# The first block's norms: tiles asked for between the next stage's products, four side by side, and one group of the modulation multiplied inside the norm

## The reference, cut to what matters

```python
def modulate(x, shift, scale): return x * (1.0 + scale) + shift
mods = adaln_modulation(c, ada_w[layer], ada_b[layer])   # silu(c) @ ada_w + ada_b, nine vectors of 1024
x = layer_norm(ALPHA * x + 0.5 * mods[2] * ffn(modulate(x, *mods[0:2])), g0, b0)
x = layer_norm(ALPHA * x + mods[5] * mixer(modulate(x, *mods[3:5])), g1, b1)
x = layer_norm(ALPHA * x + 0.5 * mods[8] * ffn(modulate(x, *mods[6:8])), g2, b2)
```

## Time and profile before

| | us |
|---|---|
| median of 3 runs | 2887.48 (2884.63 to 2893.36) |
| profiled execution | 2885.58 |
| its span | 2883.8 |
| granted clock of TensorE, mean | 0.949 |
| HBM | 348.98 MB read, 121 GB/s over the span |

### The profile page before, as it was taken

The page is one execution under the profiler, slowest core; times in us unless marked ns, Lnnn a source line. Parts: engine busy times, 40 slices in busy tenths (PEclk is TensorE's granted clock), DMA queues, the critical chain, the costliest instruction groups (busy, mean ns, idle before and its releaser), DMA issues.

```text
span 2883.8 us, 43361 instructions
## 1 busy us (share of the span) xinstructions
PE 2680.6 (93%) x16824; PEld 2313.4 (80%) x16824; DVE 1731.7 (60%) x2978; ACT 1260.8 (44%) x2390; POOL 671.8 (23%) x608
## 2 busy tenths in 40 slices
PE   8999997988788999999999988989979999899998
PEld 5887886867776888887888867789978988898888
DVE  5775666778766765556554555565544656346666
ACT  3332326531255333334333345655545575454673
POOL 1111111012134111112111121021134424555224
PEclk9999998998788999998999988999979999899999
DMA  6553441210002543433443422245524434334334
GB/s 252 184 175 115 153 154 44 81 59 2 2 16 74 179 168 127 144 128 117 161 153 124 168 81 74 81 139 184 183 88 135 145 109 133 131 132 139 117 104 138
DMA packets 115868, 352.85 MB, mean 122 GB/s; under 512 B 12752, under 2 KB 14928, under 8 KB 115280
## 3 DMA queue, kind: packets, MB, share of 16 engines
q1 hardware_dynamic: 115664, 350.08, 36.1%
HBM read 348.98 MB, written 1.05 MB: 121 GB/s over the span
## 4 chain that ended last, share of the span: by engine, by line
PE 72%; DVE 12%; ACT 7%; issue 5%; POOL 3%; DMA 1%; SPq 0%; DVEq 0%; ACTq 0%; POOLq 0%
PE ps L1570 20%; PE ps L1572 19%; PE ps L1571 19%; ACT spl L1884 2%; PE ps L1620 2%; DVE spl L2120 1%; DVE big L2330 1%; PE ps L1636 1%; DVE work L2307 1%; PE ps L1838 1%; PE ps L1630 1%; DVE work L2225 1%; ACT big L2061 1%; POOL bigr L2584 1%; PE ps L1581 1%
## 5 line engine op out<-in xcount | busy, mean ns | idle before, releaser
L1570 PE MATMUL ps<-bigr,spl 128*128 128x256 f32 (+1 forms) x3880 | 1344.2, 346 | 69.9 <-issue 21.2
L1571 PE MATMUL ps<-bigr,spl 128*128 128x256 f32 (+1 forms) x3880 | 1313.4, 339 | 0.0
L1572 PE MATMUL ps<-bigr,spl 128*128 128x256 f32 (+1 forms) x3880 | 1312.9, 338 | 0.0
L2120 DVE TENSOR_TENSOR spl<-ring,spl 128x512 fp32r<-128x512 f32 x838 | 678.0, 819 | 652.8 <-ACT spl L1884 650.2
L1884 ACT ACTIVATE spl<-ring 128x512 fp32r<-128x512 f32 x1024 | 623.6, 625 | 763.8 <-PE ps L1572 606.2
L1570 PEld LDWEIGHTS ps<-bigr,spl 128*128 128x128 f32 x3880 | 750.4, 193 | 182.3 <-issue 44.7
L1571 PEld LDWEIGHTS ps<-bigr,spl 128*128 128x128 f32 x3880 | 752.4, 194 | 75.0 <-issue 2.2
L1572 PEld LDWEIGHTS ps<-bigr,spl 128*128 128x128 f32 x3880 | 750.9, 194 | 76.4
L2584 POOL TENSOR_TENSOR bigr<-work,bigr 128x512 fp32r<-128x512 f32 (+1 forms) x200 | 210.8, 1060 | 1026.5 <-ACT bigr L1888 1026.4
L2579 POOL TENSOR_TENSOR spl<-ring,spl 128x512 fp32r<-128x512 f32 x186 | 254.3, 1369 | 361.2 <-ACT spl L1884 360.9
L1888 ACT ACTIVATE bigr<-work 128x512 fp32r<-128x512 f32 (+2 forms) x232 | 120.5, 522 | 317.9 <-DVE work L2202 169.2
(11 more groups left out here) (291 smaller groups left out, 2506.6 us busy)
## 6 DMA issues: line engine op xcount, KB each, us to landing
ring<-w_stream SPq DMA_DIRECT2D x512, 512.0 KB, 3.4
big<-w_stream SPq DMA_DIRECT2D x256, 256.0 KB, 3.0
big<-w_stream SPq DMA_DIRECT2D x16, 512.0 KB, 11.0
X<-x_t SPq DMA_DIRECT2D x2, 1024.0 KB, 13.7
cst<-consts SPq DMA_DIRECT2D x1, 1601.5 KB, 7.3
X<-mem_t SPq DMA_DIRECT2D x1, 1024.0 KB, 5.7
out_t<-X SPq DMA_DIRECT2D x8, 128.0 KB, 2.1
prm<-params SPq DMA_DIRECT2D x1, 252.5 KB, 2.7
```

Source lines behind the costliest of these rows:

```text
L1570: pe.matmul(out, hi, x[0], start=k == 0, stop=False)
L1571: pe.matmul(out, hi, x[1], start=False, stop=False)
L1572: finish(pe.matmul(out, lo, x[0], start=False, stop=k == nk - 1), tile, key if k == nk - 1 else None)
L2120: dve.tensor_tensor(lo_half(h), raw_half(h), hi_half(h), SUB).then_inc(*sig("lo", h, by="lo_dve"))
```

## The change

1. **Side by side.** `pair` becomes `side_by_side` for any number of products. After each norm four products (three in the odd mixer: key 0, query 0 with 256 columns, key 1) advance together by feature tile. The norm is an object, `Norm`; its `between` asks for tile k+1 before the products of k.
2. **Fills.** Five groups of the modulation (0,15), (0,16), (1,7), (1,16), (1,17) leave the background. Each is multiplied as 8 plain fp32 matmuls inside a norm: two before the sums, one between sums and squares, one behind the mean, four behind 1/deviation. Their weights are loaded into the place where `XM`'s low parts will stand, so the first tile's `dual` waits for the last fill.
3. **Product order.** High by high, low by high, and only then high by low, which waits for the input's low part.
4. **Residual** straight from the product's bank on DVE; X is kept multiplied by ALPHA (`first_scale` at the start; `ln_update` with gain and offset times ALPHA). The sums of X are multiplied before those of the squares.
5. **ln_update** one for every four feature tiles of later products instead of eight in a row; in the odd mixer, where no long product follows, all at once.
6. **Odd mixer.** The memory's squares behind the values by token; memory keys and queries regrouped.
7. The silu of a short convolution one convolution later; the square root's table asked for ahead of the sums.

```diff
             def linear(key, bank, free, k, nk, tile, x, need, n):
-                w.all(need, done)
+                for step, u in need:
+                    w.wait_ge(*done("dhi", u))
                 hi, lo = weights(tile)
                 pe.matmul(out, hi, x[0], start=k == 0, stop=False)
-                pe.matmul(out, hi, x[1], start=False, stop=False)
-                finish(pe.matmul(out, lo, x[0], start=False, stop=k == nk - 1), tile, ...)
+                pe.matmul(out, lo, x[0], start=False, stop=False)
+                w.all(need, done)
+                finish(pe.matmul(out, hi, x[1], start=False, stop=k == nk - 1), tile, ...)
...
+            def side_by_side(keys, ws, src, n, between=None, all_=None):
+                all_ = all_ or [banks.get() for _ in keys]
                 for k in range(len(src)):
                     if between:
                         yield from between(k)
                     hi, lo, need = src[k]
+                    for (bank, free, bi), key, w, n in zip(all_, keys, ws, ns):
                         tile = yield from take(w(k))
+                        yield "linear", key, bank, free, k, len(src), tile, (hi[:, 0:n], lo[:, 0:n]), need, n
...
+            class Norm:
+                def tile(self, k):
+                    if k == 0:
+                        yield "ln_sub", u, 0, n, mean[0], [mean[1]] + self.need
+                    if k < KD - 1:
+                        yield "ln_sub", u, k + 1, n, mean[0], [mean[1]] + self.need
+                    yield "ln_mul", u, k, n, r[0], r[1]
+                    yield "ln_mod", u, k, n, m, nxt[0], nxt[1], [nxt[2]] + mfree
+                    t = yield from dual(m[:, 0:n], XM[k][0][:, 0:n], XM[k][1][:, 0:n], self.read[k] + self.after)
+                def between(self, k):
+                    if k == 0:
+                        yield from self.tile(0)
+                    yield from self.tile(k + 1)
...
+                    bs, sfree, si = banks.get()
+                    yield from fill(2)
+                    yield "colsum", us, bs, [(accS, self.s)], n, sfree
+                    yield from fill(1)
+                    c = yield from columns(n, [(accQ, self.q)])
...
+                    yield from fill(1)
                     yield "inverse", u, col[:, 8:8 + nb], col[:, 4:4 + nb]
                     r = yield from root_spread(n, c)
+                    yield from fill(4)
...
+            def fill(l, g, k, bank, free):
+                if k == 0:
+                    w.all(free, done)
+                    w.wait_ge(*done("fill_in", l, g, KD - 1))
+                a = 96 + 4 * k
+                pe.matmul(bank, c4[:, a:a + 128], B((KD + k) * T, T), start=k == 0, stop=k == KD - 1)...
...
             def residual(u, k, n, bank, gt, need, xneed):
-                dve.scalar_tensor_tensor(x, x, ALPHA, t[:, 0:n], MUL, ADD)...
+                for s, a, b in halves(n):
+                    x = Xt[k][:, a:b]
+                    ins = dve.scalar_tensor_tensor(x, bank[:, a:b], gt[:, k, s:s + 1], x, MUL, ADD)
...
             def odd_mixer(xs, ms):
+                yield from headnorm(9, T, "kn", K[1], second)
+                tV = yield from odd_values(xs4, srcv, VK, f0)
                 for k in range(KD):
                     yield from sums.add(MX[k], [("m",)], k == KD - 1)
-                tV = yield from odd_values(xs4, srcv, VK, f0)
                 r, key, ri = yield from sums.finish(D, "eps6")
```

More of the change, by code:

```diff
@@ L461, in spread, with columns @@
                 return b, ("spread", u), bi
-            def columns(n, squares, plain=()):
+            def columns(n, squares):
                 b, free, bi = banks.get()
@@ L599, in ada_vec, with fill_load, fill, fill_end @@
                 yield from total(*prev)
+            def fill_load(l, g, free):
+                bank, bfree, bi = banks.get()
+                for k in range(KD):
+                    if not signals.at:
+                        side.append([("ada_w", (l,), 128 * k, 128, 512 * g, 512, 0)])
+                    yield "fill_load", l, g, k, pos["a"], free
+                    pos["a"] += 1
+                for k in range(KD):
+                    filler.append(("fill", l, g, k, bank, bfree))
+                filled[:] = [l, g, bank, bi]
+            def fill(n):
+                for _ in range(n):
+                    if filler:
+                        yield filler.pop(0)
+            def fill_end():
+                if not filled:
+                    return
+                l, g, bank, bi = filled
+                filled.clear()
+                row, rfree, ri = tmps.get()
+                yield "fill_row", l, g, row, bank, rfree
+                banks.give(bi, ("ada_row", l, g))
+                def turned():
+                    b, free, bi2 = banks.get()
+                    yield "fill_turn", l, g, row, b, free
+                    tmps.give(ri, ("ada_t", l, g))
+                    yield "ada_mod", l, g, 2, b
+                    banks.give(bi2, ("mod", l, g))
+                later.append(turned)
             def conditions(l, i):
@@ L631, in layer_norm, with next_norm @@
+            def next_norm(n, keep, sums, g, b, nxt):
+                norm = Norm(n, keep, g, b, nxt)
+                norm.after = [("fill", *filled[0:2], KD - 1)] if filled else []
+                yield from norm.chain(sums)
+                assert not filler
+                later.append(fill_end)
+                return norm.xs, norm
+            def layer_norm(n, sums, g, b):
                 mean, r = yield from sums.finish(D, "eps5")
                 u = new()
-                xs, ms = [("xs", u, k) for k in range(KD)], []
+                xs = [("xs", u, k) for k in range(KD)]
+                following = Sums(n, both=False, need=[pos["colsum"]])
@@ L827, in even_mixer @@
                 for n, m in enumerate((0, 4, 1, 5, 2, 6, 3, 7, 8, 9, 10, 11)):
-                    yield from qkv(m, first if n == 0 else None)
+                    yield from qkv(m, (first, second)[n] if n < 2 else None)
                     if normed:
@@ L1134, in odd_mixer @@
             def odd_mixer(xs, ms):
-                yield from flush()
+                first, first_q, second = yield from side_by_side(
+                    [("attn_in", m) for m in (8, 0, 9)], [tile_of("attn_w_in", (0,), 128 * m) for m in (8, 0, 9)], [(*XM[k], ms.m[k]) for k in range(KD)], (T, L, T), ms.between)
+                yield from run_later()
                 f0 = [("down", 2, KD - 1), pos["colsum"]]
@@ L1541, in store @@
                 sp.dma_start(OUT[:, k, 0:L], Xt[k][:, 0:L]).then_inc(*sig("stored", k, n=16))
-            run({f.__name__: f for f in (start, load, ada_load, load_memory, store)})
+            run({f.__name__: f for f in (start, load, ada_load, fill_load, load_memory, store)})
             w.wait_ge(*done("stored", KD - 1))
@@ L1604, in ada_raw, with fill_turn @@
                 finish(ins, tile, ("ada", l, g) if k == KD - 1 else None)
+            def fill(l, g, k, bank, free):
+                if k == 0:
+                    w.all(free, done)
+                    w.wait_ge(*done("fill_in", l, g, KD - 1))
+                a = 96 + 4 * k
+                pe.matmul(bank, c4[:, a:a + 128], B((KD + k) * T, T), start=k == 0, stop=k == KD - 1).then_inc(*sig("fill", l, g, k))
+            def fill_turn(l, g, row, bank, free):
+                w.wait_ge(*done("ada_row", l, g))
+                w.all(free, done)
+                for q in range(4):
+                    ins = pe.matmul(bank[:, 2 * q:2 * q + 2], row[0:2, q * 128:(q + 1) * 128], P("ident")[0:2, 0:2], start=True, stop=True)
+                ins.then_inc(*sig("ada_t", l, g))
             def ada_turn(l, gs, row, bank, free):
@@ L1899, in ada_row, with fill_row @@
                 act.activation(row[rows, :], bank[rows, :], ACTF.Copy).then_inc(*sig("ada_row", l, g))
+            def fill_row(l, g, row, bank, free):
+                w.wait_ge(*done("fill", l, g, KD - 1))
+                w.all(free, done)
+                act.activation(row[0:2, :], bank[0:2, :], ACTF.Copy).then_inc(*sig("ada_row", l, g))
             def square(u, sq, ap, need):
@@ L1911, in deviation, with sqrt_table, first_scale @@
                 act.activation(v, v, ACTF.Sqrt, bias=P(eps)).then_inc(*sig("sd", u))
-            def residual(u, k, n, t, bank, gt, need, xneed):
-                w.all(need, done)
-                for s, a, b in halves(n):
-                    ins = act.activation(t[:, a:b], bank[:, a:b], ACTF.Copy, scale=gt[:, k, s:s + 1])
-                ins.then_inc(*sig("res_t", u))
+            def sqrt_table():
+                act.activation(scratch, P("eps5"), ACTF.Sqrt)
+            def first_scale(k):
+                w.wait_ge(*done("first_mod", k))
+                act.activation(Xt[k], Xt[k], ACTF.Copy, scale=ALPHA).then_inc(*sig("x_scaled", k))
             def glu(f, m, t, bg, bu, free):
```

261 lines of the change are left out of this document (151 added, 110 removed).

## The result

The changed kernel took 2900.25 us (median of 6, 2894.28 to 2901.72) against 2886.61 of the kernel before on the same chip: ratio 1.0043, 95% interval 1.0028 to 1.0057. It is slower by 13.6 us, inside the stated range and on its upper side. The forecast of 2893 was too low by half of the change, and lay in the band (to 2896.1) that the prediction counts as no change, where the measured time lies above it.

The account below looks back on a forecast made before the run. TensorE, busy 93% of the span, was taken as the bound, with norm handovers running through several engines. Terms of +14.1 and -7.4 gave +6.7 on 2885.58; with part of the median's excess, 2893 us, range 2868 to 2907.

Parts of the forecast that it names:

- The pace of the norm loop: Norm loop: DVE's weight split waits for GpSimd's subtraction, so a tile comes every 4.46 us; unblocked it would cost 3.8.
- t0+43.1: Long norms: four products end 43.1 us after t0, the last product's end before the norm; +0.2 and +0.6 us.
- the memory's column sum: Odd mixer: PE waits for this sum behind ACT's work, 1759.8 against 1746.8; +13.0, less 2.9 of query product: +10.1 us.
- The eight fills of each group fall into pauses that are there anyway, except those counted above.: Norms: fills cost nothing beyond the first tile's wait; moving five groups off DVE saves 4.3 us of PE.
- (d): Weight ring: its lead is gone because of the fills' loads, two or three stalls of 3 us, 2900 us; chance 0.05.
- The gain is lost at once: Even mixer's first half: products end at 475.5 instead of 480.7, then PE waits for DVE's split; +1.0 us.
- the term of 1.5: Even stage: a short convolution's silu one step later lets ACT pass the next evacuation first; -1.5 us.
- Scaling X: Start: 8 ACT instructions, 5.0 us, beside 8.2 us of products already split; 0 us.
- (a): Norm loop: GpSimd doesn't hold up the split, a tile takes 3.8 us; -16 us, 2877; chance 0.16, with (b) 0.08.
- (b): Odd mixer: the memory's squares don't hold PE, ACT is through earlier; -10 us, 2883; chance 0.10, with (a) 0.08.
- (c): Norm loop: PE at half clock, twelve matmuls take 5.1 instead of 4.46 us per tile; +17 us, 2910; chance 0.11.
- (e): Norms: fills find no pause, first tile late by all eight, 3.5 us per group; 2903 us; chance 0.05.

Follow-up runs that it names:

- e7: The changed kernel with each norm tile's low part made by DVE instead of GpSimd: 2892.66 us, ratio 1.0030 against the kernel before.
- e3: The changed kernel with the low parts of weight splits inside a norm made by GpSimd, not DVE: 2860.99 us, ratio 0.9914 against the kernel before.
- e4: The changed kernel without fills, the five groups back in DVE's background: 2882.24 us, ratio 0.9992 against the kernel before.
- e6: The changed kernel with two of its five fills, (0,16) and (1,16), back in DVE's background: 2890.19 us, ratio 1.0026 against the kernel before.

## Why the prediction was right and where it was not

**Right, and shown.** The pace of the norm loop: 4.46 us a tile forecast, 4.45 measured, with the split ending 0.55 after GpSimd; e7 and e3 show the cause. The end of the fourth product at t0+43.1, measured 42.9. The last norm, +2.2, measured +1.9 (of the 1.1 that residual and moments were to save there nothing shows). A place with 7.58 us of waiting ahead of the memory's column sum (10 or more were forecast), with the cause named.

**Right by two errors.** The memory's column sum was forecast for 1759.8 and came at 1759.60. But the values ended at 1744, not at 1739.7, for the most part because of the half clock from 1725 to 1735, which was not in the sum; and from there it took 15.7 us and not 20.1, since the squares take 4.9 us when nothing else uses ACT (8.2 of the earlier trace rows were spread by other work) and ACT was through with the units sooner. The +10.3 for the stretch is so partly the memory's and partly the clock's (3.9 us, by e3 over the same matmuls).

**Mis-sized: "The eight fills of each group fall into pauses that are there anyway, except those counted above."** This step failed. The net gain was put at 4.3 us; without fills the kernel is 16 us faster. Of what they cost, the tile's wait (counted in the t0+43.1) makes 0.4 to 1.6 us in a long norm. The loads were judged against a lead of "four halves", but the fill of the even mixer is loaded in a stage where the ring is not ahead, and there it costs PE a pause of 2.6 us, and 4.4 in all up to the second norm (e4); rival (d) had the mechanism and gave it a chance of 0.05. And in the odd mixer the fill goes with 10 us at half clock. In the two nets between, where 4 groups less were to save PE some 5 us, the time from one norm's fourth product to the next norm changed by 0.5 us only; why the sums' 0.85 to 1.70 each do not show there was not settled.

**Wrong sign: the even mixer's first half.** "The gain is lost at once" did not come true: 5.6 us are kept to matmul 2112. At the fourth product's end the changed kernel is 5.6 ahead (42.9 against 48.4). Then PE stands, but for another reason and for less than the 7 us forecast. DVE's split starts 14.3 us after the fourth product (at 491.71; 15.6 was counted), and PE never waits for it. What PE waits for is a column sum behind ACT, in both programs. Before, then after:
```profile
488.00 1.02 PE L1630 MATMUL ps<-cst,work 128*128 128x1 f32 x8 [1.71 <-ACT work L1903]
```
```profile
487.71 1.87 PE L1773 MATMUL ps<-cst,work 128*128 128x1 f32 x8 [3.91 <-ACT work L2051]
```
The 132nd matmul behind the kernel before's t0 was put at about 490.5; its trace has 493.5, so that side was taken 3 us too fast. By matmul 1728 (the 144th) a lead of 1.7 us is left, where 1.0 was to be lost. The later column sums give 4.0 more, 0.4 to 1.1 at each of seven (three of them show a wait of 0.38 to 0.82 before, none after); the term of 1.5 was meant for them. The step that failed is the wait: a split that PE was to stand for, where a column sum held it.

**Missed: the start (+2.1) and the end (+3.6).** Scaling X was costed at 0 because 8.2 us of products stood ready. The cover hid the splits but not what stands behind the piece on ACT, the first silu, from there DVE's list, a modulation slot and the ring's load on SP. In the second block nothing but the square root's table moved. Its load (1.28 us at 2493.97) is gone from there in the changed kernel, so that PE starts the next products earlier and then waits longer. Before, then after, PE:
```profile
2503.72 0.50 PE L1581 MATMUL ps<-spl,bigr 128*128 128x512 f32 x1 [1.51 <-DVE spl L2120]
```
```profile
2515.40 0.50 PE L1711 MATMUL ps<-spl,bigr 128*128 128x512 f32 x1 [3.13 <-DVE spl L2270]
2517.07 0.63 PE L1711 MATMUL ps<-spl,bigr 128*128 128x512 f32 x1
```
After the longer wait the matmuls go to half clock at 2516.66 for some eight of them (0.43 apart). The kernel before has such a stretch too, but ahead of its pause (from 2496.80), where it costs nothing. So 0.9 us gained by the missing table load becomes 0.9 lost. All eleven profiles with the table change, the changed kernel's and the ten experiments', lose the same 1.6 us over these matmuls; no run puts the table load back, so the cause is argued. Another 1.1 to 1.2 us is lost in all eleven around the second block's last norm (matmuls 11900 to 12000), for a reason that no run shows.

**The rivals.** (a), a loop not held up by GpSimd, is out. (b), the memory's squares not in the way, is out. (c), half clock through the side-by-side products, did not come in the long norms (granted clock 1.00, better than the 0.80 to 0.86 of the earlier trace rows), but did in a part of the fourth (0.85, from 1707.7 to 1717.9) and behind the odd products. (d) is true at one place. (e) in part: the first tile waits for the last fill.

**Luck in the total.** That the time lies in the range is owed in part to misses of both signs: +2.1 at the start, +4.2 at the end of the even mixer, most of the 4.3 that were to be saved, and +3.6 at the end, against 5.1 too much forecast for the even mixer's first half.

## What to carry to other kernels

When work is interleaved on one in-order engine, put down for one turn of the loop which engine's list holds whose next step; the pace followed from a few rows and was right to 0.01 us here, while the cure (the step that blocks moved to the engine that has room, 37 us) was worth nearly three times what the whole change had cost. Work put "into the waits" brings its loads and its buffer's wait along: ask of each load what the queue behind it is short of at that place, not on average. And a step whose gain is read as a difference needs both sides counted to the same matmul.

## What the runs showed of the hardware

A DVE subtraction with both inputs in SBUF that starts under a GpSimd one takes 1.34 to 1.39 us instead of 0.69 and ends 0.55 after it; a half modulation (128x256) ends 0.1 to 0.15 after it. The Trainium skill ("SBUF — State Buffer", section "Who interferes with whom") calls this an exclusive lock held for the whole instruction. The trace agrees that nearly all of the later one comes behind the first, but not to the full: by the rule it would end 0.69 after GpSimd, and it ended 0.55 after it each time.

A stretch in which PE has no pause can still run at the lower clock: in the changed kernel 45 matmuls from 1725 to 1735 ran back to back at 1.2 GHz (granted clock 0.50), and the clock rose to 2.4 only then. Its last pauses before that were 0.62, 0.96 and 0.62 us. In e6 the values ran at 2.4 from the start (granted clock 1.00 from 1712.7 on), behind last pauses of 0.62, 0.94 and 0.62 us at the same matmuls, so the pauses right before don't tell the two apart.
